# Neighbourhood attention in pairs of heads: both row halves of TensorE in one step, values by half heads in one bank, one bank for the projection beside it

## What is computed

```python
def odd_mixer(h, w_qkv, rel_bias, w_out, rows):
    q, k, v = jnp.split(h @ w_qkv, 3, axis=-1)        # 16 heads of 64
    return neighbourhood_attention(q, k, v, rel_bias, rows) @ w_out

# neighbourhood_attention, for each grid row and column:
s = jnp.einsum('bchd,bacwhd->bhcaw', q_r, k_win) * scale
s = s + bias.transpose(0, 2, 1, 3)[None]
p = jax.nn.softmax(s.reshape(bsz, h, GRID_W, kh * kw), axis=-1)
return jnp.einsum('bhcaw,bacwhd->bchd', p.reshape(s.shape), v_win)
```

## Time and profile before

| what | us |
|---|---|
| median of 3 runs | 2723.18 |
| lowest and highest run | 2721.81, 2744.44 |
| span of the profiled execution | 2728.4 |
| PE busy in it | 2627.8 (96%) |
| DVE busy in it | 1199.8 (44%) |
| POOL busy in it | 1572.9 (58%) |
| first piece of the projection to first matmul of `odd2_out` | 2110.5 to 2308.7 |

### The profile page before, as it was taken

How to read it: one execution, slowest core, us unless ns; L and a number is a source line. 1 busy time by engine, 2 the same in 40 slices (tenths; PEclk the granted TensorE clock), 3 DMA queues, 4 the chain that set the end, 5 groups by cost and what they waited for, 6 DMA issues and landing times.

```text
span 2728.4 us, 32300 instructions
## 1 busy us (share of the span) xinstructions
PE 2627.8 (96%) x11402; PEld 2046.6 (75%) x11402; DVE 1199.8 (44%) x1719; ACT 602.6 (22%) x1122; POOL 1572.9 (58%) x1329
## 2 busy tenths in 40 slices
PE   7999988999999999999999999999999998999998
PEld 2876446888788886667788887888887776788886
DVE  4353656446333314657533322333213777533311
ACT  3222431112111102256211111111102344211100
POOL 2523015666666775523666776676776664666675
PEclk9999999999999999889999999999999999999999
DMA  6311432333323332100332333333332211233332
GB/s 229 126 41 60 141 121 89 100 94 98 93 92 100 100 101 76 65 1 3 101 100 93 99 102 99 95 97 95 103 102 91 74 59 40 93 100 92 100 100 85
DMA packets 69058, 249.07 MB, mean 91 GB/s; under 512 B 7664, under 2 KB 10224, under 8 KB 68336
## 3 DMA queue, kind: packets, MB, share of 16 engines
q1 hardware_dynamic: 63936, 232.81, 27.3%
q10 hardware_dynamic: 5040, 15.16, 1.6%
HBM read 245.85 MB, written 2.10 MB: 91 GB/s over the span
## 4 chain that ended last, share of the span: by engine, by line
PE 89%; DVE 6%; ACT 2%; issue 2%; DMA 1%; POOL 0%; SPq 0%; ACTq 0%; DVEq 0%; POOLq 0%
PE pb L384 68%; PE pb L830 3%; PE pb L776 2%; PE pb L705 2%; PE pb L736 1%; PE pb L791 1%; PE pb L443 1%; PE pb L552 1%; PE pb L815 1%; PE pb L800 1%; PE pb L716 1%; PE pb L425 1%; PE pb L482 1%; PE pb L525 1%; PE pb L592 1%
## 5 line engine op out<-in xcount | busy, mean ns | idle before, releaser
L384 PE MATMUL pb<-ar,w_hi 128*128 128x512 f32 x5600 | 1739.2, 392 | 10.5 <-DVE ar L1264 4.5
L384 PEld LDWEIGHTS pb<-ar,w_hi 128*128 128x128 f32 x5600 | 1049.5, 188 | 246.5 <-issue 15.3
L384 PE MATMUL pb<-ar,w_lo 128*128 128x512 f32 x2800 | 1091.2, 390 | 0.0
L300 POOL TENSOR_TENSOR w_lo<-raw,w_hi 128x1024 fp32r<-128x1024 f32 x396 | 990.7, 2502 | 33.0
L296 POOL TENSOR_TENSOR still<-still 128x1 f32<-128x1 f32 x396 | 80.2, 202 | 932.0 <-PE pb L384 627.1
L384 PEld LDWEIGHTS pb<-ar,w_lo 128*128 128x128 f32 x2800 | 526.8, 188 | 110.4
L297 POOL TENSOR_SCALAR w_hi<-raw 128x1024 fp32r<-128x1024 f32 x396 | 421.0, 1063 | 0.0
L1522 DVE TENSOR_TENSOR tb<-pb,nb 128x512 f32<-128x512 f32 x88 | 60.9, 692 | 417.8 <-PE pb L384 417.8
L1443 DVE SCALAR_TENSOR_TENSOR x<-pb,x 128x512 f32<-128x512 f32 x48 | 36.5, 760 | 381.9 <-PE pb L384 381.9
L1528 DVE TENSOR_TENSOR ar<-tb,ar 128x512 f32 x88 | 156.2, 1775 | 91.0 <-ACT ar L1077 91.0
L1077 ACT ACTIVATE ar<-tb 128x512 f32 x88 | 55.7, 633 | 531.5 <-DVE tb L1525 531.5
(11 more groups left out here) (196 smaller groups left out, 2394.0 us busy)
## 6 DMA issues: line engine op xcount, KB each, us to landing
raw<-wstream SPq DMA_DIRECT2D x444, 512.0 KB, 3.5
x<-xt ACTq DMA_DIRECT2D x2, 2048.0 KB, 9.1
rt<-nbias ACTq DMA_DIRECT2D x16, 192.0 KB, 2.4
tb<-dft ACTq DMA_DIRECT2D x1, 2048.0 KB, 8.6
out<-x ACTq DMA_DIRECT2D x8, 256.0 KB, 2.2
tb<-ctxt ACTq DMA_DIRECT2D x1, 1024.0 KB, 13.4
rt<-rope ACTq DMA_DIRECT2D x1, 1024.0 KB, 4.8
rt<-nmask ACTq DMA_DIRECT2D x1, 640.0 KB, 3.8
```

The source lines that it names most:

```text
L300: pool.tensor_tensor(w_lo[:, n % SPLIT, :], raw[:, j, :], w_hi[:, n % SPLIT, :].bitcast(F32), ALU.subtract).then_inc(s_split, 1)
L384: mm = pe.matmul(pb[:, bank, :], W[a][:, n % SPLIT, k * P:(k + 1) * P], rhs(b, k0 + k), start=(first and k == 0 and i == 0), stop=(last an ...
```

## The change

The loop runs over 32 steps w = 4hp + j (pair of heads hp, query block j). One step makes both heads of the pair, one on each half of the 64 + 64 rows.

- Scores: three passes, and in each pass one matmul for rows 0..63 and one for rows 64..127, into two banks; banks (4, 5) and (2, 3) in turn.
- Transposes of step w-2 for side 0 (bank 1), then side 1 (bank 6).
- Values by half heads: bank 7 holds the queries of one half (blocks 0 and 1, or 2 and 3) of both heads, side 0 in columns 0..255 and side 1 in columns 256..511. Each call makes nine matmuls (six over 256 columns, three over 128) instead of a quarter of twelve. The zeroed corners of the probabilities go away, with their POOL instructions.
- The values of the first side wait until both `ylo` of the half before are done. In PE's loop they come ahead of the two pieces of the projection.
- The projection uses bank 0 alone (bank 1 for its second tile only), so a tile's first matmul waits for `qk_lo` of the tile just before. 10 pieces run ahead, two per step after that.
- DVE: both `tensor_tensor_reduce`, one negation over two columns, one reciprocal over two columns, two scalings, then at even steps two `ylo` (64 x 256), then two low parts. Before, `ylo` was last.
- Biases of two heads come in one transfer (8 instead of 16), into `rt` or `nb`. POOL's `bias_mask(w)` makes two buffers (of eight) when the transposes of step w-4 are done.

```diff
-            def scores_c(u):
+            def scores_c(w):
+                hp, j = divmod(w, 4)
+                if w >= 2:
+                    pe.wait_ge(ct["mx"], w - 1)
...
                 for i, (a, b) in enumerate(PASSES):
+                    for side in range(2):
+                        rows = slice(64 * side, 64 * side + 64)
+                        mm = pe.matmul(pb[:, C_BANKS[w % 2][side], 0:(hi - lo) * P], qq[a][rows, j * P:(j + 1) * P],
+                                       kk[b][rows, lo * P:hi * P], start=(i == 0), stop=(i == 2))
...
+            def turn_c(w):
+                for side in range(2):
+                    n = 2 * w + side
+                    pe.wait_ge(ct["p"], n + 1)
+                    if n >= 2:
+                        pe.wait_ge(ct["lo"], n - 1)
...
+            HALVES = [[(1, 0, 2), (0, 0, 2), (2, 1, 2)], [(2, 2, 4), (3, 2, 4), (1, 2, 3)]]
+            def values_c(half, side):
+                hp, which = divmod(half, 2)
+                pe.wait_ge(ct["lo"], 4 * half + 2 + side + 1)
+                if side == 0 and half >= 1:
+                    pe.wait_ge(ct["ylo"], 2 * half)
...
-                    pe.wait_ge(s_ev, TILE0["odd2_qk"] + (m - 1 if m > 1 else -4))
+                    pe.wait_ge(s_ev, TILE0["odd2_qk"] + (m if m > 2 else 1 if m == 2 else -4))
...
-            for u in range(64 + 7):
-                if u < 64:
-                    scores_c(u)
-                if 3 <= u < 67:
-                    turn_c(u - 3)
-                if u + 9 < 64:
-                    qk_piece(u + 9)
-                if u >= 7:
-                    values_c(u - 7)
+            for w in range(32 + 4):
+                if w < 32:
+                    scores_c(w)
+                if 2 <= w < 34:
+                    turn_c(w - 2)
+                if w >= 4:
+                    values_c((w - 4) // 2, w % 2)
+                for n in (2 * w + 10, 2 * w + 11):
+                    if n < 64:
+                        qk_piece(n)
```

DVE's loop after the change, with its waits:

```diff
+            for w in range(32 + 5):
+                if w % 2 == 1 and (w + 3) // 2 < 16:
+                    qk_lo((w + 3) // 2)
+                if w < 32:
...
+                    dve.wait_ge(ct["s"], 2 * w + 2)
+                    dve.wait_ge(ct["bm"], 2 * w + 2)
+                    for side in range(2):
...
+                        link(dve.tensor_tensor_reduce(p, pb[:, C_BANKS[w % 2][side], 0:n], p, 1.0, -3.0e38, ALU.add,
+                                                      ALU.max, tiny[:, b + side:b + side + 1]))
+                    dve.tensor_scalar(tiny[:, 8 + c:10 + c], tiny[:, b:b + 2], -1.0, None, ALU.mult)\
+                        .then_inc(ct["mx"], 1)
+                if 1 <= w < 33:
...
+                    dve.wait_ge(ct["e"], 2 * v + 2)
+                    link(dve.reciprocal(tiny[:, 40 + c:42 + c], tiny[:, 16 + c:18 + c]))
+                    for side in range(2):
...
+                        dve.tensor_scalar(p, p, tiny[:, 40 + c + side:41 + c + side], None, ALU.mult)\
+                            .then_inc(ct["p"], 1)
+                if w >= 6 and w % 2 == 0:
+                    half = (w - 6) // 2
+                    hp, which = divmod(half, 2)
+                    dve.wait_ge(ct["yhi"], 2 * half + 2)
+                    for side in range(2):
...
+                                          O_VY[0][rows, hp, cols].bitcast(F32), ALU.subtract).then_inc(ct["ylo"], 1)
+                if 2 <= w < 34:
...
```

More of the change, by code:

```diff
@@ L158, in build, with bias_buffer @@
                  for w in range(2)] for b in range(2)]
[L160 to L170, removed]
+        O_PT = [[area(21504 + 4096 * side + 2048 * s, 4, TOK) for s in range(2)] for side in range(2)]
+        O_P = [tb[:, :, :].rearrange("p a b -> p (a b)")[:, 3 * P * i:3 * P * (i + 1)] for i in range(8)]
+        def bias_buffer(hp):
+            if hp % 2:
+                return nb[:, 0:2, :].rearrange("p a b -> p (a b)")[:, 0:6 * P]
+            return rt[:, 2:4, :].rearrange("p a b -> p (a b)")[:, 2 * P:8 * P]
         C_WIN = tb[:, 3, 0:KT * 14].rearrange("p (k c) -> p k c", k=KT)
         S_BANKS = (4, 5, 0)
-        C_BANKS = (4, 5, 3)
-        CT_BANKS = (6, 2)
+        C_BANKS = ((4, 5), (2, 3))
+        CT_BANKS = (1, 6)
         P_ROWS = (0, 1, 2, 4)
@@ L788, in scores_c @@
                 lo, hi = chunks_of(j)[0], chunks_of(j)[-1] + 1
-                qq, kk = O_QK[(h // 2) % 2]
+                qq, kk = O_QK[hp % 2]
                 for i, (a, b) in enumerate(PASSES):
[L791 to L819, removed]
+                    for side in range(2):
+                        rows = slice(64 * side, 64 * side + 64)
+                        mm = pe.matmul(pb[:, C_BANKS[w % 2][side], 0:(hi - lo) * P], qq[a][rows, j * P:(j + 1) * P],
+                                       kk[b][rows, lo * P:hi * P], start=(i == 0), stop=(i == 2))
+                        if i == 2:
+                            mm.then_inc(ct["s"], 1)
@@ new lines, in turn_c @@
+            def turn_c(w):
[4 more added lines that the diff above has]
+                        pe.wait_ge(ct["lo"], n - 1)
+                    for c in range(len(chunks_of(w % 4))):
+                        mm = pe.transpose(pb[:, CT_BANKS[side], c * P:(c + 1) * P],
+                                          O_P[2 * (w % 4) + side][:, c * P:(c + 1) * P], ident)
+                    mm.then_inc(ct["t"], 1)
@@ new lines, in _ @@
+            HALVES = [[(1, 0, 2), (0, 0, 2), (2, 1, 2)], [(2, 2, 4), (3, 2, 4), (1, 2, 3)]]
[4 more added lines that the diff above has]
+                    pe.wait_ge(ct["ylo"], 2 * half)
+                for c, (k, q0, q1) in enumerate(HALVES[which]):
+                    o0 = 2 * P * side + (q0 - 2 * which) * P
+                    for i, (a, b) in enumerate(PASSES):
+                        mm = pe.matmul(pb[:, 7, o0:o0 + (q1 - q0) * P], O_VY[a][:, hp + 1, k * P:(k + 1) * P],
+                                       O_PT[side][b][:, k, q0 * P:q1 * P], start=(c == 0 and i == 0),
+                                       stop=(c == 2 and i == 2))
+                mm.then_inc(ct["o"], 1)
@@ L850, in _ @@
                 group(m % 4, SPL0["odd2_out"] + m, lambda b, k: O_VY[b][:, k, :],
-                      (lambda k: pe.wait_ge(ct["ylo"], 2 * k + 2)) if m == 0 else None)
+                      (lambda k: pe.wait_ge(ct["ylo"], 4 * k + 4)) if m == 0 else None)
             ffn("ffn3")
@@ L1163, in qk_hi @@
                 act.wait_ge(s_group, SPL0["odd2_qk"] + m + 1)
[L1164 removed]
+                act.activation(O_QK[i % 2][w][0], pb[:, int(m == 1), :], ACT.Copy, scale=SCALE if w == 0 else 1.0)\
                     .then_inc(ct["qk_hi"], 1)
```

153 lines of the change are left out of this document (66 added, 87 removed).

## The result

| what | before | after |
|---|---|---|
| median, us | 2725.66 (4 runs) | 2794.22 (4 runs) |
| lowest to highest, us | 2721.81 to 2744.44 | 2786.41 to 2806.02 |
| ratio after / before | | 1.024 (95%: 1.0203 to 1.0277) |
| span of the profiled execution, us | 2728.4 | 2791.9 |
| PE busy in it, us | 2627.8 | 2643.3 |

The change makes the kernel 2.4% slower. The prediction said 2758 in a range of 2731 to 2790: the direction was right, the size too small.

A forecast was written before the change was run, and what follows sets the result against it. PE was taken to bound the kernel (89% of the chain). Saving -19, stall +33, small waits +2, tail +3.5, clock +15 make +34.5 on 2728.4: 2763, less 5.2 for profiling, 2758 us; range 2731 to 2790.

The forecast's parts named there:

- PE's saving: In the loop, paired scores and fewer mode changes cut PE's work from 23.28 to 20.4 us per two heads: -19 us.
- rivals on pairs and narrow matmuls: In scores and values: pairs share nothing, or 128-wide matmuls are slow; +11 or +10 us, 2768; chance 0.08.
- The stall on `ylo`: PE waits before a half's first-side values for DVE's `ylo`: 3.0 us for each of halves 1 to 11, +33 us.
- hidden: Rival: `ylo` is done when PE reaches the values, so only -19 us is left: 2704 us; chance 0.06.
- short stall: Rival: POOL's additions miss the scalings, waits before the values are 2.3 us, clock stays full: 2731 us; chance 0.17.
- Small waits: In the loop, PE's waits for `lo` before the transposes and for bank 0 before a tile: +2 us.
- The clock in the loop: Idle stretches before the values lower PE's clock, 1.0 us lost each; +15 us for 15 stretches including the tail's.
- my upper end of 25: Bound of the clock term: all 15 idle stretches of PE cost 1.7 us each, 25 us.
- The tail: Steps w = 27 to 35, behind the last pieces: 18 us of PE work plus waits, 33.2 against 29.8: +3.5 us.
- clock low throughout: Rival: clock at 0.50 through the whole phase, about 95 us more over the loop, some 2840 us; chance 0.07.
- Scalings of 0.8 us and more: Sign that the forecast is right: DVE's scalings in the changed phase take 0.8 us and more.
- Two steps about 13 us apart: Sign that the forecast is right: two steps of the changed loop lie about 13 us apart.

The follow-up runs named there:

- e10: e6 with side 0's scores before the step's transposes and side 1's behind them; 2744.28 us, 1.0042 of the kernel before.
- e1: Kernel after with the values moved behind the two pieces of projection in PE's loop, nothing else; 2725.77 us, 0.999 of the kernel before.
- e6: e5 plus a POOL wait for the last scaling ahead of the `odd2_out` weight splits; 2713.12 us, 0.9943 of the kernel before.
- e7: e6 with the scores issued as three passes of side 0, then three of side 1; 2712.14 us, 0.9951 of the kernel before.
- e4: Kernel after plus twelve overwritten 512-column matmuls on PE before the values of each even step; 2763.11 us, 1.0135 of the kernel before.
- e9: Kernel after plus eight overwritten 512-column matmuls on PE before the values of each even step; 2760.37 us, 1.0108 of the kernel before.
- e3: Kernel after with the two-column negation made as two one-column negations; 2774.53 us, 1.0183 of the kernel before.
- e5: Kernel after with values behind the pieces, two one-column negations, and `ylo` ahead of the reductions from step 28 on; 2715.23 us, 0.9959 of the kernel before.
- e8: Kernel after plus four overwritten 512-column matmuls on PE before the values of each even step; 2769.40 us, 1.0172 of the kernel before.

## Why the prediction was wrong in size

Against the profiled execution the sum was +34.5, and the phase grew by 66.0. The 31.5 between them, by steps:

- **PE's saving, forecast -19: right.** 149.4 against 168.0 us of work. Its parts held: six scores take 0.55 us (256 columns; 0.73 for 384) and the sides start 3 ns apart, so the pair shares nearly all. The values take 1.08 us to the next start, against 1.03. Its three matmuls over 128 columns take 0.06, 0.115 and 0.11 us to the next start (forecast 0.11, bounds 0.10 and 0.23). The rivals on pairs and narrow matmuls fall. By e10 nearly all of the saving, 19.9 us of work, is the pair's.
- **The stall on `ylo`, forecast 11 x 3.0 = +33: right.** All waits of L812 are 48.1 us, those in the tail 3.37, 6.84, 0.91 and 1.87, which leaves 35.1, 3.2 each. (The forecast's two chains add up to 3.04 and 2.66, where it says 3.05 and 2.65; the mean stays.) e1 shows the mechanism. With it the rivals "hidden" and "short stall" fall. Inside the chain one price was wrong: the negation was counted as 0.07 to the next start, as over one column, and took 0.83. The POOL time that it absorbed was missing at the scalings (715 ns instead of the 1046 of the earlier trace rows over 256 columns), so the sum came out right. The Trainium skill, "VectorE: DVE Perf Modes", section Mode 2×_2P, has a rule for it: a `tensor_scalar` in SBUF takes both read ports if its outermost dimension that isn't one is even, and two columns are such a dimension. The trace agrees in that two columns are held up beside POOL (870 ns in the mean) and one isn't (154). The negation at 2238.18 ends at 2239.10, and the first of POOL's two additions beside it at 2239.07.
- **Small waits, forecast +2: +8.4.** Five times, in every second pair of steps, the transposes wait about 1.0 us for DVE's low part of the transposes one step earlier (L797 on L1664; 0.98 in the timeline above), and once 1.72 us at the start. I counted this wait only by name. In the timeline of DVE above, that low part starts at 2236.79, and the step that begins at 2237.26 comes behind it.
- **The clock in the loop, forecast 11 x 1.0 = +11: +31.7.** 224.6 less 149.4 of work less 43.5 idle (33.1 with the 148.0 of e6; the saving then is 1.4 larger, and the sum stays). This is the step that failed, and it is two thirds of the miss. I took one row of a single gap (2.16 us, then 10 us at 0.83), so 1.7 us lost, as the upper bound, and discounted it because not every gap lowers the clock. Here all eleven waits in the loop had a low stretch on them or right behind them, ten of 6.8 us, with about 1.55 us of it inside the 3.37 us waits and 0.66 inside the 3.03 us ones: (6.8 - 1.1) / 2 = 2.85 us lost each. The rows of one wait of 3.37 us above show 2.4; a wait of 3.03 has 6.2 us of its stretch behind it, so 3.1. At that rate my upper end of 25 for all fifteen waits should have been 43. The bound came from a gap shorter than the ones I forecast, and the trace of before had longer ones: the 3.88 us of idle in the tail has 6.8 us at low clock (0.66 over 10 us), and in two other stretches of 10 us at 0.54 and 0.53 (1046 to 1056, 2058 to 2068) gaps of 3.70 and 4.50 us follow ones of 2.17.
- **The tail, forecast +3.5 and 4 for its clock: +9.6.** Idle time there is 15.3 us, against the 15.2 in the forecast, though in one wait of 6.84 rather than several of 3. PE's work was put at 18 us. e7, with 3.4 us of low clock, shows 30.6 - 8.5 = 22.1, less up to 1.7 for the clock, and less 1.1 for one call of values that stands ahead of the last pieces in the kernel after: about 19 to 21. That leaves 3 to 5 us for the clock, which is 19.3 us low (6.1 of it inside waits), against the forecast 4. So the work was put too low rather than the clock, but the runs don't part the two closer.

Differences: 20.7 + 2.1 (tail) + 6.4 (small waits) + 2.1 (stall) + 0.4 (saving) = 31.7, for 31.5. The rival "clock low throughout" (2840) did not come either. With full clock the kernel would stand near 2794 - 32 = 2762, and e4 and e9, whose clock is full in the loop but for 3.4 us and whose waits are filled but no shorter, stand at 2763 and 2760.

Among the signs that were to tell: 15 waits of 48.1 us in sum (forecast 40 to 50), scores in 0.55 and 0.73, clock below 1.00 were as named. "Scalings of 0.8 us and more" held over 384 columns (863 ns) and not over 256 (715). "Two steps about 13 us apart" was not: 2257.55 - 2241.37 = 16.2.

Open: why two of the waits of about 3 us in e3 draw no low clock at all, why a wait of about 1.4 us in the tail draws one in some kernels and none in others, and why e10's tail stays low.

## What to carry to other kernels

When a change moves an operation ahead of the work that used to lie before it on its engine, count the chain on the other engine against what is left as cover: here the same edits are 2.4% slower with the values ahead of two pieces and, with the values behind them and two small mends (e5), 0.4% faster than before. Price an idle gap of PE as the gap plus what the clock takes after it, and take that from gaps as long as the forecast one. Where a gap can't be removed, useless matmuls in it can be cheaper than the gap.

## What the runs showed of the hardware

- Waits of 3.0 to 3.4 us before dense matmuls, one per 16 to 18 us, cost 2.4 to 3.1 us more each through the clock, which stood at 1.2 GHz for 6.8 us around ten of eleven. In e3, with waits of 3.0 to 3.2 us, seven of nine such stretches were 3.4 us. Eight or twelve overwritten matmuls in each wait brought the granted clock in the loop back to 1.00 and made the kernel 31 to 34 us faster.
- Shorter waits can lower it too: 2.46 us did five times of five in e8, 2.12 us once of six, 1.2 and 1.6 us never in the loop of e9. In the tail a wait of 1.36 to 1.45 us was followed by none, 6.8 or 13.7 us at 1.2 GHz, depending on the kernel.
- `tensor_scalar` over 128x2 took 870 ns on average beside POOL's additions (up to 1.58 us beside a split), 0.17 us with POOL idle; over 128x1 154 ns.
- Three matmuls on rows 0 to 63 followed by three on rows 64 to 127 overlap as fully as alternating ones: 0.55 us for six, the halves starting 10 ns apart instead of 3.
- Of three matmuls over 128 columns behind six over 256, the second and third start 0.115 and 0.11 us before the next one, hardly less than the 0.117 to 0.12 of one over 256; the first takes 0.06.
